# The gate and up products of a feed-forward layer: one 512-column product for the high weight with both parts of the tokens, and five small moves of order

## The reference, cut to what matters

```python
h = rms_norm_2(x, ffn_norm_g)                # 256 x 1024
gate, up = split(h @ w_ffn_in, 2, axis=-1)   # two times 256 x 2816
x = x + (silu(gate) * up) @ w_ffn_out        # 2816 x 1024
```

## Time and profile before

| | |
|---|---|
| median of three runs | 760.7 us (759.38 to 761.69) |
| the profiled execution | 758.98 us |
| its span | 757.2 us |
| PE busy | 740.2 us, 98% |
| PEld busy | 636.8 us, 84% |
| DVE busy | 503.8 us, 67% |
| ACT busy | 380.4 us, 50% |

### The profile page before, as it was taken

The page is one execution under the profiler, slowest core; times in us unless marked ns, Lnnn a source line. Parts: engine busy times, 40 slices in busy tenths (PEclk is TensorE's granted clock), DMA queues, the critical chain, the costliest instruction groups (busy, mean ns, idle before and its releaser), DMA issues.

```text
span 757.2 us, 12205 instructions
## 1 busy us (share of the span) xinstructions
PE 740.2 (98%) x5023; PEld 636.8 (84%) x5023; DVE 503.8 (67%) x693; ACT 380.4 (50%) x577; POOL 25.7 (3%) x43
## 2 busy tenths in 40 slices
PE   5999999999999999999999999999999999999998
PEld 2687886478887777789999999999988999999886
DVE  2486769648847867785789999647963745536431
ACT  2564576645354657445533444697453444344330
POOL 3000001001000000012000000000000000000000
PEclk9999999999999999999999999999999999999999
DMA  9995448924366373353744644514452655454511
GB/s 370 421 384 175 165 168 311 404 92 146 126 238 242 112 278 113 133 211 113 277 168 167 215 176 171 191 57 145 159 200 108 243 203 196 146 215 179 211 56 55
DMA packets 21958, 146.50 MB, mean 193 GB/s; under 512 B 2588, under 2 KB 2716, under 8 KB 5392
## 3 DMA queue, kind: packets, MB, share of 16 engines
q1 hardware_dynamic: 20880, 142.62, 50.5%
q0 software_dynamic: 752, 2.06, 0.8%
q10 hardware_dynamic: 272, 1.05, 0.4%
HBM read 144.68 MB, written 1.05 MB: 192 GB/s over the span
## 4 chain that ended last, share of the span: by engine, by line
PE 80%; DVE 1%; ACT 1%; issue 0%; POOL 0%; ACTq 0%
PE banks L459 24%; PE banks L461 23%; PE banks L460 23%; PE banks L553 3%; PE banks L642 1%; PE banks L577 1%; PE banks L685 1%; DVE WL L1693 1%; PE banks L930 0%; PE banks L915 0%; PE banks L689 0%; PE banks L945 0%; PE banks L653 0%; PE banks L934 0%; PE banks L932 0%; PE banks L920 0%
## 5 line engine op out<-in xcount | busy, mean ns | idle before, releaser
L1693 DVE TENSOR_TENSOR WL<-RAW,WH 128x2048 fp32r<-128x2048 f32 (+1 forms) x103 | 233.6, 2279 | 60.6 <-ACT WH L1178 60.2
L1178 ACT ACTIVATE WH<-RAW 128x2048 fp32r<-128x2048 f32 (+1 forms) x103 | 195.8, 1907 | 73.8 <-PE banks L461 65.9
L459 PE MATMUL banks<-HH,WH 128*128 128x256 f32 x768 | 218.2, 284 | 0.0
L460 PE MATMUL banks<-HL,WH 128*128 128x256 f32 x768 | 217.3, 283 | 0.0
L461 PE MATMUL banks<-HH,WL 128*128 128x256 f32 x768 | 217.3, 283 | 0.0
L459 PEld LDWEIGHTS banks<-HH,WH 128*128 128x128 f32 x768 | 147.3, 192 | 1.1 <-issue 1.0
L460 PEld LDWEIGHTS banks<-HL,WH 128*128 128x128 f32 x768 | 147.4, 192 | 0.1
L461 PEld LDWEIGHTS banks<-HH,WL 128*128 128x128 f32 x768 | 147.3, 192 | 0.0
L459 PE MATMUL banks<-WH,HH 128*128 128x512 f32 (+1 forms) x320 | 127.5, 398 | 1.4 <-DVE WL L1975 0.4
L461 PE MATMUL banks<-WH,HL 128*128 128x512 f32 (+1 forms) x320 | 124.4, 389 | 0.0
L460 PE MATMUL banks<-WL,HH 128*128 128x512 f32 (+1 forms) x320 | 124.1, 388 | 0.0
(11 more groups left out here) (296 smaller groups left out, 908.8 us busy)
## 6 DMA issues: line engine op xcount, KB each, us to landing
RAW<-in_weights_dram SPq DMA_DIRECT2D x114, 1024.0 KB, 4.9
BIG<-in_weights_dram SPq DMA_DIRECT2D x6, 1024.0 KB, 5.9
ROTS<-in_weights_dram SPq DMA_DIRECT2D x4, 1024.0 KB, 7.4
PROBS<-in_weights_dram SPq DMA_DIRECT2D x2, 1024.0 KB, 12.3
RAW<-in_weights_dram SPq DMA_DIRECT2D x2, 816.0 KB, 11.0
GATE<-in_weights_dram SPq DMA_DIRECT2D x3, 512.0 KB, 9.8
X<-in_x_dram ACTq DMA_DIRECT2D x1, 1024.0 KB, 5.6
QT<-in_weights_dram SPq DMA_DIRECT2D x1, 1024.0 KB, 13.3
```

The lines of the kernel that those rows point to most:

```text
L459: pe.matmul(out_, lhsT=w[0], rhs=x[0], start=start, stop=False, **more)
L460: pe.matmul(out_, lhsT=w[0], rhs=x[1], start=False, stop=False, **more)
L1178: do(act.activation(WH[:, home[n], 0:kb * width], RAW[:, slot[n] % RAW_RING, 0:kb * width], ACT.Copy), high_done)
L1693: do(dve.tensor_tensor(WL[:, home[n], w], RAW[:, slot[n] % RAW_RING, w], WH[:, home[n], w], ALU.subtract), low_done)
```

## The change

`HH` and `HL` become the two halves of one tensor `HBOTH`, 2048 elements apart. In groups 2 to 10 of the feed-forward layer `by_both` replaces `by_features`: each block `b` has a PSUM bank of its own; the high weight meets high and low tokens in one matmul of 512 columns (left half of the bank: high, right half: low), and the low weight meets the high tokens in one of 256 columns that adds to the left half. DVE then adds the two halves of each bank with a `tensor_reduce`, whose input steps between the halves for each token. ACT and the multiplication now read SBUF. The gate uses the kind "proj", the up part "turn", the transposes of groups 0 and 1 go to "out".

Five other edits move work: the transposes of `n2`, token half 1, into the second half of the `k2` product; in step 6 of the first attention `normalise` ahead of `peaks` on DVE and the gate eviction ahead of the exponentials on ACT, with three extras of DVE one step on or swapped; a piece of low weights ahead of the second normalisation of `n2`; one such piece behind the first eviction of the `ato` branch.

```diff
+            def by_both(name, j, use, kind):
+                wait_parts(pe, name, j)
+                wh, wl = parts(name, j)
+                for b in range(2):
+                    bank = ps.open(pe, kind, f"{use}.{b}")
+                    both = bank[:, :].rearrange("p (u s) -> p u s", u=2)
+                    for k in range(KB):
+                        high, low = wh[:, k, b * P:(b + 1) * P], wl[:, k, b * P:(b + 1) * P]
+                        if k < KB - 1:
+                            pe.matmul(both, lhsT=high, rhs=HBOTH[:, :, k, :], start=k == 0, stop=False)
+                        pe.matmul(bank[:, 0:S], lhsT=low, rhs=HH[:, k, :], start=False, stop=False)
+                    mm = pe.matmul(both, lhsT=high, rhs=HBOTH[:, :, KB - 1, :], start=False, stop=True)
+                    ps.fill(mm, f"{use}.{b}")
...
-            norm_turn(2, 1)
-            half_tokens("k2", 1, 0)
+            half_tokens("k2", 1, 0, between=lambda: norm_turn(2, 1))
...
-                by_features(f"fi{i}", 0, use=f"fg.{i}")
+                by_both(f"fi{i}", 0, f"fg.{i}", "proj")
...
-                by_features(f"fi{i}", 1, use=f"fu.{i}")
+                by_both(f"fi{i}", 1, f"fu.{i}", "turn")
...
-                pe.wait_ge(ff_low, i + 1)
+                if i < 2:
+                    ps.wait_drained(pe, f"ht.{i}")
+                else:
+                    pe.wait_ge(ff_low, i - 1)
...
-                bank = ps.wait_filled(act, f"fg.{i}")
-                ps.drain(act.activation(ZT[:, i % 2, :], bank[:, :], ACT.Silu), f"fg.{i}")
+                for b in range(2):
+                    ps.wait_drained(act, f"fg.{i}.{b}")
+                do(act.activation(ZT[:, i % 2, :], QR[:, i % 2, :], ACT.Silu), silu_done)
...
+                    turned = layer == 0 and i == 6
+                    if turned:
+                        normalise(i - 1)
                     if i < b:
                         peaks(i)
-                    if a <= i - 1 < b:
+                    if a <= i - 1 < b and not turned:
                         normalise(i - 1)
...
-                          5: [lambda: lows(15), lambda: row_in(0, 5), lambda: lows(16)], 6: [lambda: gate(3)],
+                          5: [lambda: row_in(0, 5), lambda: lows(15)], 6: [lambda: lows(16)], 7: [lambda: gate(3)],
...
+            lows(mix_first + 4)
             gained_hat("n2", 1, MIXR)
-            lows(mix_first + 4)
...
-            lows(branch_first + 8)
...
+                if j == 0:
+                    lows(branch_first + 8)
...
-                if i >= 3:
-                    low_hidden(i - 1)
-                ps.wait_drained(dve, f"fg.{i}")
-                bank = ps.wait_filled(dve, f"fu.{i}")
-                do.after()
-                ps.drain(dve.tensor_tensor((ROT1, ROT2)[i % 2][:, :], ZT[:, i % 2, :], bank[:, :], ALU.mult), f"fu.{i}")
+                full = (ROT1, ROT2)[i % 2]
+                if i >= 4:
+                    dve.wait_ge(silu_done, i + 1)
+                for use, dst in ((f"fg.{i}", QR[:, i % 2, :]), (f"fu.{i}", full)):
+                    if dst is full and i >= 3:
+                        low_hidden(i - 1)
+                    for b in range(2):
+                        bank = ps.wait_filled(dve, f"{use}.{b}")
+                        ps.drain(dve.tensor_reduce(dst[:, b * S:(b + 1) * S], bank[:, :].rearrange("p (u s) -> p s u", u=2), AX.X,
+                                                   ALU.add), f"{use}.{b}")
+                for b in range(2):
+                    ps.wait_drained(dve, f"fu.{i}.{b}")
+                dve.wait_ge(silu_done, i + 3)
+                do(dve.tensor_tensor(full[:, :], ZT[:, i % 2, :], full[:, :], ALU.mult), hidden_made)
```

More of the change, by code:

```diff
@@ L190, in two_blocks_kernel @@
         X = sb("X", [P, NT, D])
-        HH, HL = sb("HH", [P, KB, S], F32R), sb("HL", [P, KB, S], F32R)
+        HBOTH = sb("HBOTH", [P, 2, KB, S], F32R)
+        HH, HL = HBOTH[:, 0, :, :], HBOTH[:, 1, :, :]
         CST, COL = sb("CST", [P, max(n_cst, cst["ropec"][0] + n_cst2)]), sb("COL", [P, n_cols])
@@ L315, in two_blocks_kernel @@
         merged, silu_done, stored = sem("merged"), sem("silu_done"), sem("stored")
+        hidden_made = sem("hidden_made")
         def const(name):
@@ L526, in by_features @@
                 readers[index[(name, j)]] = ps.filled_at(use)
+            def by_both(name, j, use, kind):
[11 more added lines that the diff above has]
+                    ps.fill(mm, f"{use}.{b}")
+                readers[index[(name, j)]] = ps.filled_at(f"{use}.1")
             def branch(name, j, src, ready):
@@ L1020, in hidden_turn @@
                     ps.wait_drained(pe, f"fh.{i}.{t}")
-                turn(f"ht.{i}", [ZT[:, t, i * S + b * P:i * S + (b + 1) * P] for b in range(2) for t in range(NT)])
+                turn(f"ht.{i}", [ZT[:, t, i * S + b * P:i * S + (b + 1) * P] for b in range(2) for t in range(NT)], kind="out")
             normed(3, 0)
@@ L1314, in high_heads, with attention @@
                 do(act.activation(HH[:, o, :], ZS[:, o, :], ACT.Copy), ot_high)
-            def attention(layer, extra):
+            def attention(layer, extra, first={}):
                 a, b = spans[layer]
                 for i in range(a, b + 4):
+                    for what in first.get(i - a, ()):
+                        what()
                     if i < b:
@@ L1414, in _ @@
                           5: [lambda: evict("cmpT", CPT[:, :, :], flat2), lambda: highs(16), lambda: gate_half("zb.1", 3)],
-                          6: [gate_out]})
+                          }, {6: [gate_out]})
             highs(first_split("q1_0") + 1)
@@ L1629, in high_hidden @@
             def high_hidden(i):
-                ps.wait_drained(act, f"fu.{i}")
+                act.wait_ge(hidden_made, i - 1)
                 do(act.activation(AH[:, 2 * i:2 * i + 2, :], (ROT1, ROT2)[i % 2][:, :].rearrange("p (b s) -> p b s", b=2),
@@ L1644, in _ @@
                 if i >= 4:
[L1645 removed]
+                    act.wait_ge(hidden_made, i - 3)
                 else:
                     ps.wait_filled(act, "ht.1")
[L1648 to L1649 removed]
+                for b in range(2):
+                    ps.wait_drained(act, f"fg.{i}.{b}")
+                do(act.activation(ZT[:, i % 2, :], QR[:, i % 2, :], ACT.Silu), silu_done)
                 feed(f"fi{i}", 1)
@@ L2344, in low_turned @@
                 bank = ps.wait_filled(dve, f"ht.{i}")
-                do(dve.tensor_tensor(AL[:, 2 * i:2 * i + 2, :], bank[:, :].rearrange("p (b s) -> p b s", b=2),
-                                     AH[:, 2 * i:2 * i + 2, :], ALU.subtract), ff_low)
+                ps.drain(dve.tensor_tensor(AL[:, 2 * i:2 * i + 2, :], bank[:, :].rearrange("p (b s) -> p b s", b=2),
+                                           AH[:, 2 * i:2 * i + 2, :], ALU.subtract), f"ht.{i}")
             def low_hidden(i):
```

1 line of the change is left out of this document (removed).

## The result

The kernel after takes 756.25 us (median of 6 runs, 754.56 to 757.67), the kernel before 760.53 us in the same comparison (6 runs, 759.26 to 761.69). The ratio is 0.9944, 95% interval 0.9931 to 0.9957: faster by 4.3 us, 0.56%, beyond the 0.3% that can be told from no change. The forecast was 754.9 us with 750.5 to 760.0.

The account below looks back on a forecast made before the run. The prediction took TensorE's (PE's) stream as the bound. Gains of 3.7 (wide matmul) + 0.60 + 0.57 + 0.9 (pauses) = 5.8 us took 760.7 to 754.9 us, whole range 750.5 to 760.

Parts of the forecast that it names:

- The wide matmul: Feed-forward groups 2 to 10: a block step goes from 360 to 347 ns (227 + 120), 288 steps, 3.7 us gained.
- outer bound: Feed-forward block steps: alternating widths might cost up to 10 ns a step, 2.9 us lost; given little weight.
- The low end of 7 ns a step: Feed-forward block steps: with 233 ns for the wide matmul, 7 ns a step is saved, 2.0 us.
- The reductions: DVE in the feed-forward loop: four more reductions a group, turn 11.2 against PE's 11.1 us, costing nothing under cover.
- The cover of 4.4 us: Feed-forward loop: first gate bank drained about 6.7 us into a group, wanted by PE at 11.1; seven turns use 0.7.
- the rival: DVE's strided PSUM reductions run slower than the rows say; 7.5 to 11.2 us lost, priced at 764 us; chance 0.17.
- The pauses: PE's waits at 132.0, 336.6 and 536.2 us go through moves of order; gains 0.9, 0.57 and 0.60 us.
- the two late ones: PE's waits at 336.56 (low part of `k2`) and 536.17 us (bank of `ato`); gains 0.57 and 0.60 us.
- the first: PE's wait at 132.01 us for scaled probabilities of pair 5: 1.35 us go, 0.9 taken because this part lives on DMA.
- A step that nears 334 ns: Rival, feed-forward block step: narrow weight loads fit beside wide matmuls, 227 + 107, 7.5 us gained, 751.1 us; chance 0.11.
- A step that is not shorter: Rival, feed-forward block step: no gain there, the pauses alone give 2.1 us, 758.6 us; chance 0.10.
- inner range: Whole kernel: the forecast's own range, 752.3 (5.5 + 2.5) to 757.5 us (2.0 + 1.2); forecast chance 0.62.

Follow-up runs that it names:

- e12_all_wide: Kernel after, with the low weight also taking both token parts in 512 columns; stage 124.21 us, against 96.67 in after.
- e5_grouped: Kernel after, with each block's eight 512-column matmuls first, then its eight 256-column ones; 755.59 us in one execution, stage 95.84 us.
- e9_chains: Kernel after, with each piece's sixteen wide matmuls over two banks first, then its sixteen narrow ones; 755.68 us, ratio 0.9953 to before.
- e4_swap: Kernel after, with wo0_1 in step 12 and the conditioning columns in step 13 of the first attention, swapped; 754.85 us, ratio 0.9933 to before.
- e7_two_banks: Kernel after, with two wide matmuls (one into each bank), then two narrow ones, in turn; 755.7 us at full clock, stage 95.62 us.
- e10_chains_swap: Kernel after, with sixteen wide then sixteen narrow matmuls a piece, and wo0_1 and the conditioning columns swapped in the first attention; 755.79 us, ratio 0.9950 to before.

## Why the prediction was right, and where it was not

**The bound.** Right. PE's stream and its stops account for the whole change: 4.57 us from the parts, 4.65 together at full clock.

**The wide matmul: mis-sized.** The term was 3.7 us with 227 ns behind the wide and 120 behind the narrow matmul; it measured 2.2 (288 x 7.7 ns). Both durations were right for chains of one width (226.7 in e12_all_wide, 120 in the earlier trace rows). What failed is the step that put them side by side. The prediction named a cost of alternating widths as an outer bound, up to 10 ns a step, and gave it little weight "since no row shows such a change of width in a long chain"; it is 5.6 ns, shown by e12_all_wide, which has no change of width and no excess, and by e5_grouped and e9_chains, where fewer changes leave less of it. The low end of 7 ns a step came from the 233 ns of the second layer, and its 2.0 us come near the measured 2.2 by luck: those matmuls have no change of width, and why they take 233 is open.

**The reductions: right.** Strides between two halves of a bank cost nothing (683 against 681 ns), the turn of DVE was 11.38 against a worked out 11.2, and it fell behind PE by 0.11 us a group (0.1 forecast). That 0.11 and 0.1 agree so well is partly luck: DVE's turn and PE's were both some 0.17 us longer than worked out. The cover of 4.4 us, which only an added load can show, held to 0.1 us with four more reductions and to 0.4 us with one more. The rule that made the rival, in the Trainium skill's Advanced Engine Details and Errata, Memory Cachelines, is not borne out for this read of PSUM by VectorE (683 ns); the section states the penalty for every access in a new line of SBUF, and for PSUM it speaks of matmuls.

**The pauses: right.** 1.3 us for the two late ones (1.17 forecast), 1.1 for the first (0.9). There the reason given for the discount was only partly it: what is left is a wait for the exponentials on ACT (0.37), which the prediction did not name. PE does not wait for `ROTS` near 149 us in after's profile, where only a weight load waits for it, 0.5 us; in that of e4_swap PE waits 0.4 us.

**The rivals.** A step that nears 334 ns: the other way round, since next to a wide matmul a narrow one takes 117 instead of 120 but the wide one 235 instead of 227. A step that is not shorter: no, 352 ns. The formula in the Trainium skill's TensorE: Matmul & The Clock Gate, Back-to-back issue gap, makes 216 and 109 ns; the section gives it for the isolated gap, and in these chains, where each matmul has a weight load of its own, one width keeps 226.7 and 120 ns, as in the kernel before.

**Slips in the working.** The busy time of DVE in a group, put at 9.0 us, adds up to 8.2 from the prediction's own terms, and 8.19 was measured in the turn from 612.37 to 623.75. The upper corner of its inner range, 5.5 + 2.5 us, is 752.7 us and not 752.3. Neither changes the forecast.

**The median.** 5.8 us forecast, less 1.5 for the wide matmul, plus 0.4 for the pauses, is 4.7, what executions at full clock show. The medians differ by 4.3, as they mix executions with a fall of the clock and without. That before has them as well I had not read from its three times (759.38, 760.7, 761.69), which are 2.3 us apart, with a profile that had none.

## What to carry to other kernels

A pace read from a chain of equal matmuls holds for such a chain; where shapes take turns, price the turn, or put equal widths in a row as far as the banks allow (348 to 349 ns a step here with two, eight or sixteen in a row, 352 with one). When work is added to an engine that is not the bound, write its loop as one chain with its hand-overs, compare the turn with the bound's, and count the cover in us: here busy shares (70%) said nothing, and the chain was right to 0.1 us for four more reductions and to 0.4 for one more. A new order of matmuls is also a new order of bank requests: two banks asked for at once cost 1.95 us at the one place where the second was late, more than the order gave everywhere else.

## What the hardware showed that was not expected

- Behind a change from 256 to 512 columns five or six wide matmuls start 233, 236, 228, 233, 231 and 226 ns apart before the pace is 226.7; behind the change back the first narrow one takes 113 instead of 120. Together 20 ns for a change in both directions, in the long rows of e5_grouped and e9_chains. Where the rows are shorter a change in both directions costs less: 3.2 ns in e7_two_banks (two in a row), 5.6 in after. What makes it is open.
- The granted clock fell to 0.50 for 3 to 4 us in eight of fourteen profiles, each time in the first attention, near 111 us, near 160 or at both, up to 2 us behind a run of matmuls of 2 or 15 columns. (The lower level in the last microsecond of some programs is not counted.) All fourteen have these runs of matmuls, so they are not enough to bring it about. PE of e10_chains_swap ahead of its fall at 111 us:

```profile
107.98 1.96 PE L802 MATMUL banks<-V,QT 64*128 64x15 f32 x32
109.78 0.91 PE L660 MATMUL banks<-KT,QT 64*128 64x128 f32 x8
110.62 0.50 PE L671 MATMUL banks<-MASK 128*128 128x256 f32 x2
```

```profile
110.00:111.00 1.00, 1.00 (x10) 0.58 (x8) 0.93 (x3) 1.00 (x3) 0.00 (x0) 1.00 0.00 0
111.00:112.00 1.00, 0.86 (x6) 0.58 (x6) 0.97 (x4) 0.11 (x1) 0.00 (x0) 0.61 0.00 0
112.00:114.00 2.00, 2.00 (x14) 0.66 (x14) 1.84 (x6) 1.58 (x8) 0.00 (x0) 0.50 0.04 8
```

  The same program has the fall in one execution and not in the next, so it is no property of an order of instructions alone. One costs some 1.5 us, a third of what this change brings.
